# A two-layer streaming encoder on one core: output projection, norm and routing of a token tile issued between the attention groups of later tiles

## The reference, cut to what matters

```python
mod = silu(c) @ w_ada + b_ada                 # shift, scale, gate for mixer and experts
h = rms_norm(x, g_norm_mix) * (1 + sc_a) + sh_a
q, k, v, iq, ik, iw, u = split(h @ w_in)
# A: an indexer scores the keys, the best k_top stay, softmax attention over them
# B: a, b = split(u); g = a*sigmoid(b); causal depthwise conv (31) -> layer_norm -> silu
x = x + gt_a * (concat(A, B) @ w_out)          # output projection
h = rms_norm(x, g_norm_ffn) * (1 + sc_f) + sh_f
# router: best of 4 groups, best 2 of its 4 experts; SwiGLU experts of width 256
x = x + gt_f * moe(h)
```

## Time and profile before

| | us |
|---|---|
| runs | 1494.12, 1496.53, 1491.05 (median 1494.12) |
| the profiled execution | 1492.04 |
| its span | 1490.2 |
| PE busy | 1258.9 (84%) |
| DVE busy | 548.7 (37%) |
| ACT busy | 368.6 (25%) |
| POOL busy | 151.9 (10%) |
| mean granted PE clock | 0.904 of 2.4 GHz |

### The profile page before, as it was taken

The page is one execution under the profiler, slowest core; times in us unless marked ns, Lnnn a source line. Parts: engine busy times, 40 slices in busy tenths (PEclk is TensorE's granted clock), DMA queues, the critical chain, the costliest instruction groups (busy, mean ns, idle before and its releaser), DMA issues.

```text
span 1490.2 us, 16205 instructions
## 1 busy us (share of the span) xinstructions
PE 1258.9 (84%) x6299; PEld 739.5 (50%) x6299; DVE 548.7 (37%) x1394; ACT 368.6 (25%) x838; POOL 151.9 (10%) x218
## 2 busy tenths in 40 slices
PE   4998799987899879999709987998787995999980
PEld 0572244543445467777505733544455454777750
DVE  1106689023345521111151058960423454211114
ACT  2124110035741111111131142001468111111113
POOL 0401050010000160000021014110100011000002
PEclk9998899987999879999958989999858996999995
DMA  9248996261950589999560310224030026799975
GB/s 362 63 146 290 363 332 201 72 228 35 312 184 34 189 289 371 365 362 368 179 230 0 123 59 29 72 66 138 20 76 3 1 97 206 254 363 362 366 248 190
DMA packets 137126, 284.99 MB, mean 191 GB/s; under 512 B 11565, under 2 KB 91861, under 8 KB 130649
## 3 DMA queue, kind: packets, MB, share of 16 engines
q1 hardware_dynamic: 116416, 209.70, 41.9%
q0 software_dynamic: 8352, 42.50, 8.2%
q10 hardware_dynamic: 12281, 31.74, 6.0%
HBM read 237.91 MB, written 52.40 MB: 195 GB/s over the span
## 4 chain that ended last, share of the span: by engine, by line
PE 69%; DVE 11%; DMA 7%; ACT 6%; issue 4%; SPq 1%; ACTq 1%; POOL 0%; DVEq 0%; POOLq 0%
PE ps L476 46%; PE ps L765 9%; PE ps L486 5%; PE ps L623 3%; PE ps L684 3%; DMA W<-in_w_gate 2%; ACT arena L1106 2%; DMA X<-in_x_sample 2%; SPq L395 1%; DVE arena L1409 1%; PE ps L506 1%; DVE arena L1460 1%; PE ps L584 1%; DVE arena L1370 1%; DMA arena<-y_d,sid 1%
## 5 line engine op out<-in xcount | busy, mean ns | idle before, releaser
L476 PE MATMUL ps<-W,arena 128*128 128x256 f32 (+1 forms) x1280 | 345.5, 426 | 8.2 <-ACT arena L1212 2.8
L476 PEld LDWEIGHTS ps<-W,arena 128*128 128x128 f32 x1280 | 240.9, 192 | 82.8 <-issue 53.8
L476 PE MATMUL ps<-W,hT 128*128 128x512 f32 (+5 forms) x640 | 197.2, 468 | 6.3 <-DVE gt L1289 6.3
L486 PE MATMUL ps<-C,arena 128*128 128x128 f32 (+3 forms) x851 | 125.3, 292 | 61.5 <-DMA arena<-x_d 14.4
L476 PEld LDWEIGHTS ps<-W,hT 128*128 128x128 f32 (+1 forms) x640 | 103.4, 183 | 100.2 <-issue 86.4
L486 PEld LDWEIGHTS ps<-C,arena 128*128 128x128 f32 (+3 forms) x851 | 102.7, 155 | 97.8 <-issue 31.6
L765 PE MATMUL ps<-W,hT 128*128 128x512 f32 (+1 forms) x320 | 144.8, 607 | 5.7 <-ACT hT L1163 5.7
L476 PE MATMUL ps<-hT,W 128*128 128x64 f32 (+1 forms) x512 | 142.6, 440 | 7.1 <-ACT arena L1029 7.1
L476 PEld LDWEIGHTS ps<-hT,W 128*128 128x128 f32 x512 | 79.0, 193 | 72.1 <-issue 64.2
L765 PEld LDWEIGHTS ps<-W,hT 128*128 128x128 f32 (+1 forms) x320 | 57.1, 184 | 80.0 <-issue 73.6
L1672 DVE TENSOR_TENSOR arena<-arena,ps 128x256 f32<-128x256 f32 x32 | 13.5, 421 | 213.9 <-ACT arena L1204 213.9
(11 more groups left out here) (244 smaller groups left out, 1112.1 us busy)
## 6 DMA issues: line engine op xcount, KB each, us to landing
W<-in_w_ada SPq DMA_DIRECT2D x48, 1024.0 KB, 7.0
W<-in_w_gate SPq DMA_DIRECT2D x32, 1024.0 KB, 10.6
W<-in_w_up SPq DMA_DIRECT2D x32, 1024.0 KB, 13.0
W<-in_w_down SPq DMA_DIRECT2D x32, 1024.0 KB, 7.6
arena<-x_d SPq DMA_DIRECT2D x33, 512.0 KB, 11.1
y_d<-arena ACTq DMA_DIRECT2D x33, 512.0 KB, 7.2
W<-in_w_in SPq DMA_DIRECT2D x16, 1024.0 KB, 8.4
arena<-arena SPq DMA_DIRECT2D x128, 79.2 KB, 2.1
```

What stands on the lines that cost most here:

```text
L476: ins = T.matmul(out, l, r, start=n == 0, stop=n == len(pairs) - 1, skip_group_check=True)
L486: count(T.transpose(o, i, ident[0:m, 0:m]), done if n == len(outs_ins) - 1 else None)
```

## The change

- `ATTN` becomes 4, 3, 2, 1, 0. Tile x of the projection, norm and routing is now the x-th of this order.
- In the attention loop, group n also carries half a tile's projection (n >= 2), a tile's norm and turn (n >= 5) and its routing (n >= 6); `places` and `slots` follow at odd n from 7. Each is written into the PE, ACT and DVE streams at the place the diff shows. Only the projection of the last tile, the norm of the last two and the routing of the last three stay behind the loop.
- To free banks, logits use two banks instead of three, all products with v and the turned rows of the first three tiles share bank 5, and `logits` is issued as two halves around the products with v.
- `normalised` (the reciprocal and four multiplications by it) is DVE's alone.
- The LayerNorm branch ends in groups 0 and 1 instead of after group 9; the gate and norm vectors are loaded before group 0.
- Layer 0's ada steps of thirds 2 to 4 (24, called `later`) all stand in the convolution stage, and the loads are ordered anew; a u_block's two column sets share one slot. `conv(3)` comes before the transposes of the conv state and of the keys.
- HR of tile x has the buffers 0, 1, 0, 2, 3; POOL also stores each tile's rows to h_d, and reads them back from there if there is a further job.
- The fill DMAs are issued by POOL at the start.

```diff
-ATTN = (0, 4, 3, 2, 1)
+ATTN = (4, 3, 2, 1, 0)
...
-        HR = part(5120, 5120, NT, D)
+        HR = [part(at, 1024) for at in (17336, 18360, 17336, 0, 1024)]
+        spare = part(5120, 5120, NT, D)
...  SP, layer 0
+                    u_columns(0)
+                    later(range(0, 4))
+                    u_columns(1)
+                    later(range(4, 8))
+                    u_columns(2)
+                    shifted(0)
+                    later(range(8, 12))
+                    u_columns(3)
+                    shifted(1)
+                    later(range(12, 17))
+                    shifted(2)
+                    later(range(17, 18))
+                    shifted(3)
+                    later(range(18, 24))
+                    columns(6)
+                    columns(7)
...  PE, convolution stage
                 u_block(0)
-                ada3(0)
+                later(*range(0, 4))
                 u_block(1)
-                ada3(1)
+                later(*range(4, 8))
                 conv(0)
                 u_block(2)
-                ada3(2, 3)
+                later(*range(8, 12))
                 conv(1)
                 u_block(3)
-                ada3(4, 5)
+                later(*range(12, 16))
                 conv(2)
-                ada3(6)
+                later(*range(16, 20))
+                conv(3)
+                later(*range(20, 24))
...
-                conv(3)
-                ada3(7)
...  PE, values(n)
+                    pe.wait_ge(L["pta"], PT0[n] + len(chunks_of(t)))
+                    pe.wait_ge(*((L["on"], n) if n >= 1 else (L["lnr"], 1)))
+                    if n >= 5:
+                        pe.wait_ge(L["hTa"], n - 4)
...  PE, the loop and what follows it
+                logits(0, range(4))
+                logits(1, range(4))
+                pe.wait_ge(L["lnsq"], 1)
...
+                for n in range(len(GROUPS)):
+                    x = (n - 5) // 2
+                    turn_p(n)
+                    if n + 2 < len(GROUPS):
+                        logits(n + 2, range(2))
+                    if n >= 5 and n % 2 == 1:
+                        turn_h(x, 0)
+                    if n >= 6 and n % 2 == 0:
+                        route_tile(x)
+                    values(n)
+                    if n + 2 < len(GROUPS):
+                        logits(n + 2, range(2, 4))
+                    if n >= 2:
+                        project_out(n // 2 - 1, n % 2, (0, 1))
+                    if n >= 5 and n % 2 == 1:
+                        turn_h(x, 1)
+                    if n >= 7 and n % 2 == 1:
+                        places(x - 1)
+                project_out(4, 0, (0, 1))
+                route_tile(2)
+                project_out(4, 1, (0,))
+                for q in range(2):
+                    turn_h(3, q)
+                project_out(4, 1, (1,))
+                places(2)
+                route_tile(3)
+                places(3)
+                for q in range(2):
+                    turn_h(4, q)
+                route_tile(4)
+                places(4)
...  ACT, the loop (before it: exps(0), exps(1), the root of lnb, nine DMA issues)
+                    for q, (c, kn) in enumerate(chunks_of(t)):
...                      # copies of the transposed probabilities
+                    if n >= 4 and n % 2 == 0:
+                        square_rows((n - 4) // 2)
+                    if n >= 5 and n % 2 == 1:
+                        turned_h(x, 0)
                     if n + 2 < len(GROUPS):
                         exps(n + 2)
+                    outputs(n)
+                    if n == 1:
+                        act.wait_ge(L["lny"], 1)
...                      # four Silu
+                    if n >= 5 and n % 2 == 1:
+                        turned_h(x, 1)
...  DVE, the loop
+                    if n + 1 < len(GROUPS):
+                        normalised(n + 1)
+                    if n == 0:
...                      # reciprocal of lnb, product with cy
+                    if n + 2 < len(GROUPS):
+                        masked(n + 2)
...
+                    if n >= 4 and n % 2 == 0:
+                        normed((n - 4) // 2)
+                    if n >= 6 and n % 2 == 0:
+                        choose((n - 6) // 2)
+                    if n >= 2:
+                        gated(n // 2 - 1, n % 2)
+                    if n >= 7 and n % 2 == 1:
+                        slots((n - 7) // 2)
+                normed(3)
+                gated(4, 0)
+                choose(2)
+                gated(4, 1)
+                normed(4)
+                slots(2)
+                choose(3)
+                slots(3)
+                choose(4)
+                slots(4)
...  POOL
                     for k in range(2):
-                        scatter(t, k, sid1, s_xs)
+                        scatter(HR[x], t, k, sid1, s_xs[x % 2])
+                    pool.dma_start(h_d[t * P:t * P + rows_of(t), :], HR[x][0:rows_of(t), :]).then_inc(s_hd, 16)
```

More of the change, by code:

```diff
@@ new lines, in later @@
+                def later(ns):
+                    for n in ns:
+                        lm, q = THIRDS[2 + n // KC]
+                        k = n % KC
+                        load(later_use(n), wada[lm, :, k:k + 1, 2048 * q:2048 * q + 2048])
+                for c in range(3):
+                    columns(c)
+                if l == 0:
+                    ada(U_ADA1, 0)
+                    ada(U_ADA2, 1)
+                columns(3)
+                if l == 0:
+                    u_columns(0)
[14 more added lines that the diff above has]
+                    columns(7)
+                else:
+                    for i in range(4):
+                        u_columns(i)
+                    columns(6)
+                    shifted(0)
+                    load(mixer_use(l, 7, 0), wout[l, :, 0:4, 512:1024])
+                    load(mixer_use(l, 7, 1), wout[l, :, 4:8, 512:1024])
+                    for i in range(1, 4):
+                        shifted(i)
@@ L802, in _ @@
-                assert not done_units
-                route_tile(NT - 1)
-                places(NT - 1)
-                for t in range(NT):
-                    ins = T.matmul(ps[4][:, 180:180 + NE], ones[0:rows_of(t), :], assigned(t), start=t == 0, stop=t == NT - 1,
+                    at = 100 + NE * t
+                    out = ps[place_bank(t)][0:m, at:at + NE]
+                    pe.wait_ge(L["assign"], x + 1)
+                    if x >= 1 and x != 2:
+                        pe.wait_ge(L["sid"], x)
@@ new lines, in places @@
+                    ins = T.matmul(out, ones[:, 0:m], C[:, K_E16:K_E16 + NE], start=True, stop=False, skip_group_check=True)
+                    count(ins, None)
+                    for b in ATTN[:x]:
+                        count(T.matmul(out, ones[0:rows_of(b), 0:m], route[0:rows_of(b), R_AS + NE * b:R_AS + NE * b + NE], start=False,
+                                       stop=False, skip_group_check=True), None)
+                    count(T.matmul(out, C[0:m, K_UT:K_UT + m], assigned(t), start=False, stop=True, skip_group_check=True), L["pos"])
@@ new lines, in _ @@
+                project_out(4, 0, (0, 1))
[9 more added lines that the diff above has]
+                    turn_h(4, q)
+                assert not done_units or True
+                route_tile(4)
+                places(4)
+                for n, t in enumerate(ATTN):
+                    ins = T.matmul(ps[4][:, 0:NE], ones[0:rows_of(t), :], assigned(t), start=n == 0, stop=n == NT - 1,
@@ new lines, in _ @@
+                    if n == 1:
+                        act.wait_ge(L["lny"], 1)
+                        for c in range(4):
+                            S.activation(hT[:, 4 + c, :], cy[:, c, :], ACT.Silu, bias=vT[:, 48 + c:49 + c],
+                                         scale=vT[:, 44 + c:45 + c]).then_inc(L["mixy"], 1)
+                    if n >= 5 and n % 2 == 1:
+                        turned_h(x, 1)
+                square_rows(3)
+                for q in range(2):
+                    turned_h(3, q)
@@ L1187, in _ @@
+                square_rows(4)
+                for q in range(2):
+                    turned_h(4, q)
                 act.dma_start(gt[:, 0, :], mrows[0, 5].broadcast_to([P, D])).then_inc(L["gtf_ld"], 16)
```

461 lines of the change are left out of this document (204 added, 257 removed).

## The result

The changed kernel takes 1533.69 us (median of 4 runs, 1529.16 to 1535.52), the kernel before 1495.32 beside it: a ratio of 1.0265, 95% interval 1.0245 to 1.0284. The forecast was 1518 with the range 1486 to 1538. The profiled execution took 1535.05 us with a span of 1533.2, that is 43.0 more than the span of before.

The account below looks back on a forecast made before the run. Attention was taken as bound by ACT and the PE, DVE, ACT round trip, convolution and projection by PE. Layer 0 (21 + 1 - 2.4 + 5) and layer 1 (3 - 2.4) gave +25 us: 1518, range 1486 to 1538.

Parts of the forecast that it names:

- Part 1: Layer 0: ada steps 8 to 23 leave attention for the convolution stage; cost +15.4 us, nothing saved in the loop.
- Part 2: SP's order in layer 0's convolution stage: waiting and reordering 5.7 us, making T (first LayerNorm mean product) +21 with moved steps.
- Layer 1's +3: Transposes moved behind conv(3) no longer stand in its wait for shifted rows: +3 us, bounds 0 to 5.
- Part 3: Early fill of x_d and y_d can delay outputs that ACT waits for: +1 us, bounds -1 to +5.
- Part 4: Attention, projection and routing interleaved, from T to the experts: 210.0 against 212.4 us, -2.4 per layer.
- The early walk: Engine queues followed through layer 1's first attention groups: nmx(2) at T + 36.4, first half tile projected by T + 74.
- Part 5: Layer 0's experts: POOL reads 2.36 MB of h_d back before its second scatter; +5 us, bounds 0 to 8.
- signs of being wrong: Ada steps beside idle PE, a first group loop of 10 us, or the last projection before T + 168.
- (a): Early attention groups don't suffer from split logits and ACT's order: -17 us per layer, 1489 in all; chance 0.18.
- (b): Each of eight later attention groups pays one more 1.5 us hand-over between engines: 24 us, 1542; chance 0.10.
- (c): Only a move: the interleave gains what the moved ada steps cost, 10 us per layer, 1499; chance 0.14.
- the 3 us: Divides moved to DVE would hold back scatters and h_d stores, some 3 us more per layer; left out.

Follow-up runs that it names:

- e2: The last eight ada steps of layer 0 moved into attention groups 0 and 1 of the changed kernel, shifted(3) issued earlier: 1523.19 us, 1.0200.
- e6: Changed kernel with the transposes of conv state and keys back ahead of conv(3): 1528.37 us, 1.0221 of the kernel before.
- e1: Changed kernel with only the fill of x_d and y_d back at its old, later place: 1527.06 us, 1.0232 of the kernel before.
- c4: Changed kernel with fill late, eight steps in attention, transposes, turn_h(4) and Silu earlier, no h_d, logits of groups 2 and 3 whole: 1474.54 us.
- e4: Changed kernel with all four logits of every group n + 2 issued ahead of values(n): 1552.18 us, 1.0391 of the kernel before.
- e7: Changed kernel with ACT's four Silu behind the copies of group 0 instead of behind outputs(1): 1525.41 us, 1.0212.
- e3: Changed kernel with POOL's five loads of h_d left out, so the further job's rows aren't the normed ones: 1527.00 us, 1.0222.
- e9: Changed kernel without h_d, its stores and re-read; buffers moved so all five tiles' rows stay until the second scatters: 1519.14 us, 1.0177.
- e8: Changed kernel with ACT doing exps(n + 1) instead of exps(n + 2) behind the copies of group n: 1575.18 us, 1.0548.

## Why the prediction was right, and where it was off

The direction, the likeliest case and the range held; the time came 15.7 us above 1518. By its own steps:

**Part 1, +15.4 for sixteen steps.** Shown for eight of them by e2: they cost their full length in the convolution stage, and in the early groups nothing that shows (T to the experts 210.3, 209.8 without them). The bound "0 if the new stage hid them" is out.

**Part 2, T of layer 0 +21.** Measured +23.4 for parts 1 and 2, with the wait of 5.72 us and its cause where the walk put them. Layer 1's +3 came as +3.2 (from the end of the last u_block to T 26.7 us before and 29.9 after; 27.7 to 30.0 in the profiles with this order), and e6 gave it back (24.7).

**Part 3, the fill, +1.** This term was mis-sized: 7.4. The text named the mechanism (outputs that ACT waits for) and then took a value near nothing because PE needed no load before 113 us. What it lacked was the next step: which wait of ACT has a store behind it, and how long that store takes when weight loads, late behind the fill, keep the DMA engines full (1.01 between 110 and 118 us, 0.73 in e1).

**Part 4, -2.4 per layer.** Measured -2.1 and -1.1, but as the sum of two errors, and within what such a stretch spreads: that it agrees so well is luck. The last projection ended at T + 174.4 and 175.7, not 179.5; the tail took 35.4 and 35.8, not 30.5. The early walk was close: nmx(2) at T + 37.0 (36.4), nmx(3) at T + 50.5 (51), first projection done at T + 73.3 (74). The groups bound by PE ran faster than priced. In the tail, choose(3) ended 10.3 us behind the last projection, as walked (10.8), and the rest came late piece by piece: places(3) took 2.5 us (1.3 in the walk), turning and routing tile 0 took 6.2 us (1277.17 to 1283.40) where the walk had 3.8, places(4) and slots(4) 3.9 (2.9), and the last piece to the first transposes 9.4 (8.1). The routing's products above ran at the lower clock behind the wait, which the walk left out. One reason in the text fell: it named the split of the logits as what keeps the early groups slow. Whole logits are worth some 3 us at most, and only early (c4); in all groups they cost 8 to 10 a layer (e4). What held the early groups was above all where ACT does Silu (e7, 3 to 6.5 a layer).

**Part 5, h_d, +5.** Too small: the stage is 9.9 us shorter in e3 and 12.0 in e9, outside the bounds of 0 to 8. By the whole times it is 6.7 in e3, and 9.7 in e9 once 4.9 for HR's reuse are taken off, so the size lies near 7 to 12. The forecast priced the bytes at the rate of the stage. What it lacked is that the read-back holds back POOL's ten scatters by 14.5 us, into the load of a weight that PE needs next (18.6 us to landing instead of 12.9). Why one issue of SP is held for 13.74 us was not taken apart; PE does not wait for what stands behind it.

**Signs.** T of layer 0 came at 349.9 instead of near 340, by the fill and part 2; the last projection near T + 175 instead of T + 180, the tail at 35 instead of 30. None of the signs of being wrong appeared.

**Rivals.** (a), overlap pays: its tests at nmx(2) and nmx(3) spoke against it, rightly. (b), engines locking each other to the end: not in this kernel, where PE was busy for 105.3 of the 109.3 us from the first to the last projection; e8 shows that it is one line away. (c) had the right size for the interleave, 10 a layer, but it took mended queues to get it; its 1499 does not follow from that size, for ten instead of 2.4 in two layers is 15 us, 1503.

**The shared port.** The Trainium skill (SBUF — State Buffer, section "SBUF: two separate sides") says that DVE and GpSimd share an exclusive port pair, and that GpSimd can't write the descriptors of a DMA that it starts while DVE runs an operation in a 2-port perf mode. It adds that a DVE operation with two inputs in SBUF, as both of normed's have, takes the pair as well against a GpSimd operation that reads SBUF. No row of before showed POOL held. One of after is longer beside DVE's work; POOL of layer 1, then DVE:

```profile
1249.35 1.01 POOL L1847 DMA_INDIRECT x_d<-arena,sid  x1 [21.39 <-DVE sid L1634]
1250.66 1.48 POOL L1847 DMA_INDIRECT x_d<-arena,sid  x1 [0.30 <-issue]
```

```profile
1250.01 1.28 DVE L1590 SCALAR_TENSOR_TENSOR arena<-X,small,arena 128x1024 f32<-128x1024 f32 x1
1251.33 1.23 DVE L1591 TENSOR_TENSOR arena<-arena 128x1024 f32<-128x1024 f32 x1
```

The scatter beside normed's two wide operations takes 1.48 us (1.47 in layer 0), the others ahead of the experts 0.91 to 1.01. The trace agrees with the rule in kind, though no run tests it; but it is half a microsecond once per layer, on a tile whose HR buffer is not used again in the layer. The divides held up nothing that the runs show. The forecast's choice to leave the 3 us out stands.

## What to carry to other kernels

An interleave that fills idle time of the bounding engine is judged with its side edits: here the overlap gained nothing clear as built (1 to 2 us a layer in the profiles) and 10 to 15 once the order in its queues was mended, each fault a wait of 3 to 8 us in one engine's rows. Ask of every moved or added DMA which store or load shares the engines with it, or is held back by it, and who has a wait on that one; "PE has no idle time there" doesn't make it free. Fill work that needs little of the other engines belongs where the round trip binds; there it can be free and even raises the clock of what follows, while the stage that is full of PE charges every microsecond.

## What was not expected of the hardware

- A 16 KB store landed in 13.1 us with the DMA engines at 1.01 over the 8 us behind its issue, and in 7.1 with them at 0.73.
- A single load of 512 KB held SP's queue for 13.74 us while POOL's ten scatters were under way, and a 1 MB weight issued just ahead of it landed in 18.6 us instead of 12.9.
- Half-idle PE is charged at both ends: the routing products of one tile took 1.94 us straight behind the projection and 3.60 behind a wait of 7.58; sixteen projection products took 7.08 us in a gapless run and 7.94 to 9.10 in groups 2 to 8 of e8, with PE waits of 1.9 to 3.5 us between them.
- The steps of e2 in the idle groups took 1.92 to 2.40 us a pair and raised the granted clock over those groups from 0.70 to 0.85.
